# Final projection as seven block products of half size, 512 columns each

## What is computed

```python
def first_block(...):
    ...
        h = rmsnorm(x, norm_ffn[i])
        x = x + (jax.nn.silu(h @ w_gate[i]) * (h @ w_up[i])) @ w_down[i]
    return rmsnorm(x, final_norm)

def second_block(...):
    ...
        merged = jax.nn.sigmoid(m_a) * y_a + jax.nn.sigmoid(m_b) * y_b
        x = x + rms_norm(merged @ w_out, norm_post)
    return x
```

## Time and profile before

| | |
|---|---|
| median of 3 timed runs | 1589.2 us (1589.14 to 1589.49) |
| the profiled execution, its own time | 1593.1 us |
| its span in the trace | 1591.3 us |
| TensorE busy | 99% of the span |
| VectorE, ScalarE, GpSimd busy | 64%, 44%, 8% |
| mean granted TensorE clock | 0.997 of full speed |
| DMA over the span | mean 96 GB/s |

### The profile page before, as it was taken

How to read it: one execution, slowest core, us unless ns; L and a number is a source line. 1 busy time by engine, 2 the same in 40 slices (tenths; PEclk the granted TensorE clock), 3 DMA queues, 4 the chain that set the end, 5 groups by cost and what they waited for, 6 DMA issues and landing times.

```text
span 1591.3 us, 23787 instructions
## 1 busy us (share of the span) xinstructions
PE 1581.3 (99%) x8772; PEld 1329.7 (84%) x8772; DVE 1020.7 (64%) x1507; ACT 704.6 (44%) x1257; POOL 130.6 (8%) x121
## 2 busy tenths in 40 slices
PE   9999999999999999999999999999999999999998
PEld 7877888999988877778999998887777778888887
DVE  7666678888832466777888873437666657556444
ACT  6333345666622345544566662322455642233222
POOL 2000200000010100030000001114111012000000
PEclk9999999999999999999999999999999999999999
DMA  6422333333323331133333333252111111333332
GB/s 224 147 79 80 100 103 109 97 103 105 123 91 104 71 107 42 41 113 97 114 100 101 110 108 110 81 210 71 58 62 54 45 56 40 88 106 94 104 94 92
DMA packets 44750, 152.56 MB, mean 96 GB/s; under 512 B 5659, under 2 KB 8956, under 8 KB 44284
## 3 DMA queue, kind: packets, MB, share of 16 engines
q1 hardware_dynamic: 43888, 149.32, 30.2%
q10 hardware_dynamic: 780, 2.13, 0.5%
HBM read 149.04 MB, written 2.39 MB: 95 GB/s over the span
## 4 chain that ended last, share of the span: by engine, by line
PE 96%; DVE 2%; issue 1%; ACT 1%; DMA 0%; POOL 0%; SPq 0%; DVEq 0%; POOLq 0%; ACTq 0%
PE ps L2318 20%; PE ps L2320 20%; PE ps L2319 20%; PE ps L2526 7%; PE ps L2525 7%; PE ps L2524 7%; PE ps L2834 1%; PE ps L2856 1%; PE ps L2822 1%; PE ps L2953 1%; PE ps L2952 1%; PE ps L2954 1%; PE ps L2630 1%; PE ps L2663 1%; PE ps L2648 1%
## 5 line engine op out<-in xcount | busy, mean ns | idle before, releaser
L1365 DVE TENSOR_TENSOR w_lo<-raw,w_hi 128x1024 fp32r<-128x1024 f32 (+4 forms) x190 | 247.8, 1304 | 141.7 <-ACT w_hi L811 141.0
L811 ACT ACTIVATE w_hi<-raw 128x1024 fp32r<-128x1024 f32 (+4 forms) x190 | 199.9, 1052 | 309.0 <-PE ps L2320 275.2
L2318 PE MATMUL ps<-a_hi,w_hi 128*128 128x512 f32 x632 | 256.2, 405 | 0.7 <-DVE t L1400 0.4
L2320 PE MATMUL ps<-a_hi,w_lo 128*128 128x512 f32 x632 | 247.4, 391 | 0.0
L2319 PE MATMUL ps<-a_lo,w_hi 128*128 128x512 f32 x632 | 247.1, 391 | 0.0
L2318 PEld LDWEIGHTS ps<-a_hi,w_hi 128*128 128x128 f32 x632 | 119.0, 188 | 32.6 <-issue 7.8
L2320 PEld LDWEIGHTS ps<-a_hi,w_lo 128*128 128x128 f32 x632 | 119.0, 188 | 26.0
L2319 PEld LDWEIGHTS ps<-a_lo,w_hi 128*128 128x128 f32 x632 | 119.3, 189 | 22.0
L2524 PE MATMUL ps<-mixed_hi,t_hi 128*128 128x256 f32 x384 | 108.7, 283 | 0.0
L2525 PE MATMUL ps<-mixed_lo,t_hi 128*128 128x256 f32 x384 | 108.7, 283 | 0.0
L2526 PE MATMUL ps<-mixed_hi,t_lo 128*128 128x256 f32 x384 | 108.7, 283 | 0.0
(11 more groups left out here) (425 smaller groups left out, 3648.7 us busy)
## 6 DMA issues: line engine op xcount, KB each, us to landing
raw<-w SPq DMA_DIRECT2D x134, 512.0 KB, 3.6
raw<-w8b SPq DMA_DIRECT2D x70, 512.0 KB, 3.6
raw<-w_down SPq DMA_DIRECT2D x32, 704.0 KB, 4.0
w<-cmp_w SPq DMA_DIRECT2D x2, 2048.0 KB, 10.8
raw<-w_out_first SPq DMA_DIRECT2D x8, 320.0 KB, 2.8
raw<-w_nsa_o SPq DMA_DIRECT2D x8, 256.0 KB, 2.6
out<-o_t SPq DMA_DIRECT2D x8, 256.0 KB, 2.0
x<-xT SPq DMA_DIRECT2D x7, 256.0 KB, 6.4
```

Of the source, the lines that this page charges most:

```text
L811: act.activation(w_hi[:, slot, 0:w], raw[:, raw_slot, 0:w], ACT.Copy)\
L1365: dve.tensor_tensor(w_lo[:, slot, 0:w], raw[:, raw_slot, 0:w], w_hi[:, slot, 0:w].bitcast(F32), ALU.subtract).then_inc(w_lo_ready, 1)
L2318: pe.matmul(o, wh, a_h, start=start and at == 0, stop=False)
L2320: ins = pe.matmul(o, wl, a_h, start=False, stop=stop and at == kt - 1)
```

## The change

The 1024 x 1024 weight and the 1024 inner rows of `merged` are cut into halves, and the final projection is made from seven products of half-size blocks in place of eight (the scheme of Strassen in Winograd's form). Call A the merged input (tokens x inner rows) and B the weight (inner rows x columns); A11 is the first half of the tokens and of the inner rows, A12 the first half of the tokens and the second of the inner rows. The first half of the inner rows is the even tiles of 128, the second the odd ones; a pair p is two neighbouring tiles of `merged` (2p and 2p + 1) and the two rows 2p and 2p + 1 of `w_last`.

- **The products**, in this order: `b11` (A11 with a loaded block), `t3`, `t2`, `b21` (A12 with a loaded block), `t1`, `t4`, `b22`. Each has 4 inner tiles, 2 token tiles, 512 columns and 3 matmuls. A product's weight block is two stripes of 512 KB, each holding two inner tiles: 14 stripes, N_END = 269. `b11`, `b21` and `b22` read the weight itself (`w_blocks`, laid out beforehand); `t1`, `t2`, `t3` and `t4` are sums of weight blocks.
- **The sums of weight blocks** are made in the last down projection, whose loop is replaced by `down_beside_rows`, written out turn by turn. ScalarE loads the rows of three pairs ahead of the first turn, VectorE makes two subtractions in each half turn of the first four turns (`row_sums`), ScalarE stores them to a DRAM tensor `block_spill` in the third and fifth turn, waits there for the stores of each turn to be complete (`spill_out`), and loads the fourth pair's rows between. SyncE loads the sums back as stripes.
- **The sums of blocks of `merged`** (`part`, four of 128 x 256 for each pair) are made by VectorE behind every fourth of the last 16 strips, rounded by ScalarE (`part_high`) and completed by VectorE (`part_low`). Those of pair 3 come behind the last strip, inside the last `epilogue`.
- **Accumulators.** Two products share banks with what they are added to: ScalarE copies banks 2:4 to 4:6 behind `b11` and 4:6 to 6:8 behind `t2`, and holds `t3` in `held_t3`; VectorE adds `held_t3` to banks 4:6 and to banks 0:2. The last four strips of the second block use banks 4 to 7.
- **Operand slots.** The stripes have six slots for high and low parts (`fin_hi`, `fin_lo`) in place of two and two.
- **The ends** come in the order of tokens 2, 3, 0, 1. The last product, `b22`, goes token tile by token tile.
- Two semaphores are merged into others; `row_in` and `spill_out` are new.

```diff
+BLOCKS = ["b11", "t3", "t2", "b21", "t1", "t4", "b22"]
+LOADED = ["b11", "b21", "b22"]
+SPILLED = ["t1", "t3", "t4", "t2"]
+PAIRS = KT // 2
+PAIR_ORDER = [0, 2, 1, 3]
+DONE_ORDER = [(0, 0), (1, 0), (2, 1), (3, 1), (2, 0), (3, 0), (0, 1), (1, 1)]
+TOKEN_ORDER = [2, 3, 0, 1]
+OUT_BANK = {(0, 0): 2, (1, 0): 3, (2, 0): 4, (3, 0): 5, (0, 1): 6, (1, 1): 7, (2, 1): 0, (3, 1): 1}
...
+            sp.wait_ge(spill_out, 16 * 2 * PAIRS)
+            for j in range(LAST_STRIPS):
+                kind, half = BLOCKS[j // 2], j % 2
+                if kind in LOADED:
+                    block = a["w_blocks"][LOADED.index(kind), half]
+                else:
+                    block = spill[SPILLED.index(kind), half].rearrange("p q s -> p (q s)")
+                load(N_FIN + j, (N_FIN + j) % RAW, block, 2 * S)
...
+            def load_rows(p):
+                for k, row in ((2 * p, even_row[p]), (2 * p + 1, odd_row[p])):
+                    act.dma_start(row[:], a["w_last"][k]).then_inc(row_in, 16)
+            def spill_rows(p):
+                act.wait_ge(sums_ready, rows_summed(p, 3))
+                for c, row in ((0, even_row[p]), (2, odd_row[p])):
+                    act.dma_start(spill[c:c + 2, p // 2, :, p % 2, :].rearrange("c p s -> p c s"),
+                                  row[:].rearrange("p (c s) -> p c s", c=2)).then_inc(spill_out, 16)
+            def down_beside_rows(n0, q0, v, g, r0):
+                act.wait_ge(blk_done, n0)
+                for p in PAIR_ORDER[:3]:
+                    load_rows(p)
+                for m in range(KT):
+                    n, j = n0 + 2 * m, m % 2
+                    count = (m // 2 + r0 + 1 + j) * 16
+                    split(n + 2, KT * P if m == KT - 1 else SLOT, 0, (2 * j + 2) % 4, count)
+                    if m == 2:
+                        spill_rows(0)
+                        spill_rows(2)
+                        act.wait_ge(spill_out, 16 * 4)
+                        load_rows(3)
+                    if m == 4:
+                        spill_rows(1)
+                        spill_rows(3)
+                        act.wait_ge(spill_out, 16 * 8)
+                    residual(m, q0 + m, v, g, j, first=m < 2)
+                    split(n + 3, KT * P if m == KT - 1 else SLOT, 1, (2 * j + 3) % 4, count)
...
+            for j in range(3):
+                block_high(j)
+            epilogue(N_FIN - 1)
+            block_high(3)
+            part_high(PAIRS - 1)
+            for j in range(4, 7):
+                block_high(j)
+            act.wait_ge(lin_read, out_index(N_FIN - 1) + 1)
+            act.wait_ge(blk_done, N_FIN + 2)
+            act.activation(ps[:, 4:6, :], ps[:, 2:4, :], ACT.Copy).then_inc(seeded, 1)
+            for j in range(7, 10):
+                block_high(j)
+            act.wait_ge(blk_done, N_FIN + 4)
+            act.wait_ge(sums_ready, parts_made(PAIRS - 1) + 5)
+            act.activation(held_t3[:], ps[:, 0:2, :], ACT.Copy).then_inc(seeded, 1)
+            block_high(10)
+            act.wait_ge(blk_done, N_FIN + 6)
+            act.activation(ps[:, 6:8, :], ps[:, 4:6, :], ACT.Copy).then_inc(seeded, 1)
+            for j in range(11, LAST_STRIPS):
+                block_high(j)
...
+            def row_sums(p, steps):
+                even, odd = even_row[p], odd_row[p]
+                b11, b12, b21, b22 = even[:, 0:S], even[:, S:D], odd[:, 0:S], odd[:, S:D]
+                dve.wait_ge(row_in, 16 * 2 * (PAIRS if p == 3 else 3))
+                for step in steps:
+                    if step >= 2:
+                        dve.wait_ge(sums_ready, rows_summed(p, 0 if step == 2 else 2))
+                    o, x0, x1 = ((b11, b12, b11), (b12, b22, b12), (b22, b22, b11), (b21, b21, b22))[step]
+                    dve.tensor_tensor(o, x0, x1, ALU.subtract).then_inc(sums_ready, 1)
...
+            def parts(p):
+                first, second = tmp[:, 2 * p % 4, :], tmp[:, (2 * p + 1) % 4, :]
+                a11, a21, a12, a22 = first[:, 0:HS], first[:, HS:S], second[:, 0:HS], second[:, HS:S]
+                made = parts_made(p)
+                dve.wait_ge(prod_ready, 12 + 2 * p + 2)
+                dve.tensor_tensor(part[:, 0, :], a21, a22, ALU.add).then_inc(sums_ready, 1)
+                dve.tensor_tensor(part[:, 2, :], a11, a21, ALU.subtract).then_inc(sums_ready, 1)
+                dve.wait_ge(sums_ready, made + 1)
+                dve.tensor_tensor(part[:, 1, :], part[:, 0, :], a11, ALU.subtract).then_inc(sums_ready, 1)
+                dve.wait_ge(sums_ready, made + 3)
+                dve.tensor_tensor(part[:, 3, :], a12, part[:, 1, :], ALU.subtract).then_inc(sums_ready, 1)
...
+            for j in range(3):
+                block_low(j)
+            epilogue(N_FIN - 1)
+            block_low(3)
+            part_low(PAIRS - 1)
+            for j in range(4, 11):
+                block_low(j)
+            dve.wait_ge(seeded, seeds(3))
+            dve.tensor_tensor(ps[:, 4:6, :], ps[:, 4:6, :], held_t3[:], ALU.add).then_inc(seeded, 1)
+            block_low(11)
+            block_low(12)
             dve.wait_ge(decay_in, 16 * 2)
-            for b in range(TB):
-                post_gain(b, 0)
+            post_gain(0, 0)
+            post_gain(1, 0)
+            block_low(13)
+            dve.wait_ge(blk_done, N_FIN + 10)
+            dve.tensor_tensor(ps[:, 0:2, :], ps[:, 6:8, :], held_t3[:], ALU.add).then_inc(seeded, 1)
+            post_gain(2, 1)
+            post_gain(3, 1)
+            for i, b in enumerate(TOKEN_ORDER):
                 post_variance(b)
-                post_gain(b, 1)
-                post_add(b)
+                post_gain(b, int(b < 2))
+                post_add(i, b)
...
+            def block_rows(j, tiles_of, bank, q, t, start, stop):
+                wh, wl = (v[j % 6][:, q * S:(q + 1) * S] for v in (fin_hi, fin_lo))
+                p, o = 2 * (j % 2) + q, ps[:, bank + t, :]
+                mh, ml = tiles_of(p, t)
+                pe.matmul(o, mh, wh, start=start and p == 0, stop=False, skip_group_check=True)
+                pe.matmul(o, mh, wl, start=False, stop=False, skip_group_check=True)
+                return pe.matmul(o, ml, wh, start=False, stop=stop and p == PAIRS - 1, skip_group_check=True)
+            def block_product(kind, tiles_of, bank, start=False):
+                for half in range(2):
+                    j = 2 * BLOCKS.index(kind) + half
+                    pe.wait_ge(w_lo_ready, N_FIN + j + 1)
+                    for q in range(2):
+                        for t in range(2):
+                            ins = block_rows(j, tiles_of, bank, q, t, start, True)
+                    ins.then_inc(blk_done, 1)
+            def final_products():
+                pe.wait_ge(x1_turned, KT)
+                pe.wait_ge(zl_ready, GH + 2 * KT - 1)
+                block_product("b11", plain_tiles(0, 0), 2, start=True)
+                pe.wait_ge(sums_ready, parts_made(PAIRS - 1) + 5)
+                block_product("t3", part_tiles(2), 0, start=True)
+                pe.wait_ge(seeded, seeds(1))
+                block_product("t2", part_tiles(1), 4)
                 pe.wait_ge(zl_ready, GH + 2 * KT)
-                for b in range(TB):
-                    for i in range(KT - 3, KT):
-                        if b == 0:
-                            pe.wait_ge(w_lo_ready, N_FIN + i + 1)
-                        for h in range(2):
-                            ins = final_tile(i, b, h)
-                            if i == KT - 1:
-                                ins.then_inc(fin_done, 1)
+                block_product("b21", plain_tiles(1, 0), 2)
+                pe.wait_ge(seeded, seeds(3))
+                block_product("t1", part_tiles(0), 6)
+                pe.wait_ge(seeded, seeds(4))
+                block_product("t4", plain_tiles(1, 1), 4)
+                pe.wait_ge(w_lo_ready, N_END)
+                pe.wait_ge(seeded, seeds(5))
+                for t in range(2):
+                    for j in (LAST_STRIPS - 2, LAST_STRIPS - 1):
+                        for q in range(2):
+                            ins = block_rows(j, part_tiles(3), 6, q, t, False, True)
+                    ins.then_inc(fin_done, 1)
```

198 lines of the change are left out of this document (119 added, 79 removed).

## The result

| | kernel before | changed kernel |
|---|---|---|
| median | 1589.6 us (11 runs, 1588.74 to 1589.95) | 1593.7 us (11 runs, 1592.41 to 1597.77) |
| ratio | | 1.0028 (95% interval 1.0020 to 1.0036) |
| profiled execution: own time, span | 1593.1, 1591.3 | 1594.0, 1591.5 |

I had forecast 1586.2 in a range of 1585.0 to 1589.3. The measured time lies 4.4 us above the range. What happened is the mechanism of rival 3, ScalarE's wait for its own stores ahead of a residual, to which I had given a chance of 0.09.

What follows compares the result with a forecast made beforehand. TensorE, busy 99% of the span, bounds the kernel. From 1589.2 us: -5.44 matmuls, +1.0 hand-over, +1.0 ends, +0.4 down projection sum to -3.0, giving 1586.2 us, range 1585.0 to 1589.3.

Steps and rivals of the forecast that it cites:

- rival 3: Down projection: ScalarE waits for its stores ahead of a residual TensorE needs; 1595.6 us at 200 GB/s; chance 0.09.
- Matmuls removed, -5.44: Final projection: 168 matmuls in place of 192, 24 x 0.2267 us less on TensorE, -5.44 us.
- Hand-over, +1.0: Final projection, ahead of the second product: TensorE waits for VectorE's `part_lo` of pair 3, +1.0 us.
- Seeds, held product, operand slots at 0: Final stage: bank copies, held `t3`, its additions and six operand slots are hidden beside the products, cost 0.
- Ends, +1.0: Behind the last product: four sets of ends queue on VectorE, 2.15 us each, costing +1.0 us.
- First turn, 0 to 1.2: Last down projection: VectorE waits for six row loads ahead of the residual, 0 to 1.2 us, at worst 1.8.
- Rival 1: All DMA work of the down projection is hidden: 1585.8 us; chance 0.24.
- Third turn, "0, at most 0.8": Last down projection: four stores down at 980.1, two issues, then the residual's copy, due by 981.0; cost 0, at most 0.8.
- A gap of 2 us or more at this place: Sign against the prediction: a TensorE gap of 2 us or more in the down projection; under 1 us was expected.
- Fifth turn, 0.6 in hand: Last down projection: the same wait for stores as in the third turn without the issues, 0.6 us in hand.
- What lies around the span, 0: Outside the trace: differences in the trace were taken off the median 1589.2, with no term for time around the span.

Runs made afterwards that it cites:

- the kernel with one pair a turn: Changed kernel with slots of its own for every pair of rows, one pair loaded, summed and stored per turn: 1586.8 us, ratio to before 0.9977.

## Why the prediction was wrong, point by point

- **Matmuls removed, -5.44: right.** 24 from 192, and the distance is the same: (1550.81 - 1545.59) / 23 = 0.227.
- **Hand-over, +1.0: right.** `part_lo` of pair 3 starts 5.16 behind the first matmul (forecast 5.14), and `t3` starts at 1552.03 where 1551.04 was due: 0.99. The kernel with `mg_lo` moved showed that VectorE's queue was the cause.
- **Seeds, held product, operand slots at 0: right.** TensorE has no other gap between 1545.59 and 1584.57.
- **Ends, +1.0: right.** The last additions start 3.06 behind the last matmul in place of 1.96. Four sets follow one another at 2.2; the last additions start 42.0 behind the first matmul (forecast 41.8). Taking `t4` by tiles removed 1.1.
- **First turn, 0 to 1.2: at its lower end, in part by luck.** VectorE waited 2.89 for the loads, until 948.33, but the deadline was 949.2 (948.8 in this trace, where TensorE is 0.4 ahead of the rows of before). The loads went out from 935.79 on, when ScalarE had just started the first of the 11 `g_hi_b` copies, so ten that stand ahead of the load in the program were unstarted (rows below): the queue's lead was at least ten instructions, where the rows of before had shown three. Rival 1 was right here. The Trainium skill (Advanced Engine Details and Errata, Engine Queue Depths) gives ScalarE a queue of eight; this trace does not bear it out, since with eight the first load could not have gone out before 936.6. The price of the loads was too low, though: 12.5 us from the first issue to the last landing, where I had 10.9. The 9.1 in it was the time of the 2048 KB load alone, and two weight loads (issued at 937.46 and 945.61) fell into it, not one. Sent out at 939.5, as with a lead of three, they would by that have landed at 952.0, an estimate, 2.8 behind the deadline. The long lead hid the mistake that the third turn showed.

```profile
935.52 0.62 ACT L1114 ACTIVATE g_hi_b<-g_raw 128x512 fp32r<-128x512 f32 x1
935.79 0.36 ACTq L1177 DMA_DIRECT2D even_row<-w_last  x1
936.04 0.63 ACT L1114 ACTIVATE g_hi_b<-g_raw 128x512 fp32r<-128x512 f32 x1
...
938.64 2.70 ACT L1114 ACTIVATE g_hi_b<-g_raw 128x512 fp32r<-128x512 f32 x5
...
948.33 0.69 DVE L1912 TENSOR_TENSOR even_row<-even_row 128x512 f32<-128x512 f32 x1 [2.89 <-DMA odd_row<-w_last]
```

- **Third turn, "0, at most 0.8": the step that failed.** I took 5.3 for the stores, 1.3 fixed and one weight load of 1.8. Two loads fell into the time, and each cost 2.5: the stores were down at 983.54 and not at 980.1, 12.1 us in place of 8.4, a stop of 3.5. Of the 3.7 that were missing, 3.3 are the loads (12.1 - 7.0 - 1.8) and 0.4 the stores by themselves (7.0 - 6.6). The trace of before has both loads at 970.80 and 974.92, within my own 971.7 to 980.1; I did not look. The run with cut loads gives back all of it. A gap of 2 us or more at this place was the sign that I had named for being wrong.
- **Fifth turn, 0.6 in hand: failed by the same step.** Down 10.8 behind the first issue (1006.69 to 1017.5), a stop of 1.5.
- **What the sum had no term for:** the clock behind a stop, some 1.6. A stop of TensorE was priced at its own length.
- **What lies around the span, 0: wrong by 0.7**, and its cause is open.
- **Rival 3: the right mechanism, with its price from the wrong end.** I had it begin to decide where a pair of spills takes 3.6 us over its 5.3, and put that down to slow stores. The stores by themselves were near my price (7.0 for four of them against 6.6); what was missing were the transfers beside them. By its own working, with 3.7 more in the third turn and 2.4 in the fifth, less the 0.1 and 0.6 in hand, it gives stops of 3.6 and 1.8; 3.5 and 1.5 were measured. What made me give it 0.09 was a rate (395 GB/s) that I held against a requirement of 240, without asking who else would use it.

## What to carry to other kernels

An engine that waits for its own store to be complete, to write over the source, should issue the store a whole turn ahead of the wait: in the kernel with one pair a turn the same 4.2 MB of stores stopped nothing. Here it was even enough to move two of each four stores up by one turn, which was worth 6.7 us. Count every transfer that falls into the time of a wait, not the one that stands next to it, and add to a stop of TensorE the time at a lower clock behind it. Where the profiled execution's own time is off the median, find the place first: here 3.4 us of lower clock made two spans look equal that were 3.6 us apart (1591.5 and 1587.9).

## What was not expected of the hardware

- Around stops of 2.1, 3.5, 8.6 and 7.4 us TensorE was granted 0.50 for some microseconds, around those of 1.1 and 1.5 us it was not; the loss was 1.7 us behind the first, 1.6 behind the second and 4.1 behind the other two together. So the shorter stop cost no less clock than the longer one. That is six stops in three traces. A low clock also came with no stop of this kind: 0.52 for 7 us in the profiled execution of before, with TensorE busy. Two of 31 executions of the kernel before took 1595.8 and 1596.0 us at mean clocks near 0.995, and one of ten with two stores earlier took 1590.5 at 0.997; no trace shows where they lost it. What sets it off there stays open. The runs of the changed kernel, with two stops, spread over 5.4 us and have mean clocks of 0.996 to 0.999; those without a stop mostly spread over 1 to 2.
- ScalarE's queue issued a DMA with ten of its engine's instructions still unstarted ahead of it.
- Own time less span differs between kernels by 0.7 to 1.0 us, and in some of them from run to run, with the same span.
